# One sink exponential per banded step, a probability copy split between two engines, and final scales at other places of the queue

## The reference, cut to what matters

```python
def swa_core(q, k, v, mask, sink):
    s = jnp.einsum('bnqkgd,bnskd->bnkgqs', q, k).astype(jnp.float32) * (HEAD_DIM ** -0.5)
    s = jnp.where(mask[None, :, None, None], s, -jnp.inf)
    sk = sink.astype(jnp.float32)[None, None, :, :, None, None]
    m = jnp.maximum(jnp.max(s, axis=-1, keepdims=True), sk)
    p = jnp.exp(s - m)
    denom = jnp.sum(p, axis=-1, keepdims=True) + jnp.exp(sk - m)
    w = (p / denom).astype(v.dtype)
    return jnp.einsum('bnkgqs,bnskd->bnqkgd', w, v)

y_prompt = rmsnorm(hp, g_final)
y_sample = rmsnorm(hs, g_final)
```

## Time and profile before

| | us |
|---|---|
| median of 3 runs | 1824.55 (1822.61 to 1825.99) |
| the profiled execution's own time | 1830.64 |
| its span, first to last instruction | 1828.8 |
| PE busy in the span | 1745.8 (95%) |
| DVE, ACT, POOL busy | 879.7, 547.3, 179.6 |
| mean granted TensorE clock | 0.990 |

### The profile page before, as it was taken

How to read it: one execution, slowest core, us unless ns; L and a number is a source line. 1 busy time by engine, 2 the same in 40 slices (tenths; PEclk the granted TensorE clock), 3 DMA queues, 4 the chain that set the end, 5 groups by cost and what they waited for, 6 DMA issues and landing times.

```text
span 1828.8 us, 29483 instructions
## 1 busy us (share of the span) xinstructions
PE 1745.8 (95%) x11905; PEld 1612.9 (88%) x11905; DVE 879.7 (48%) x1707; ACT 547.3 (30%) x1216; POOL 179.6 (10%) x355
## 2 busy tenths in 40 slices
PE   6998989997898999989999999999999999999997
PEld 6997989886787999988799999999999999999996
DVE  5556656665466345124323644444444444444445
ACT  5123344576555123025402422111111222112212
POOL 2113322112122001100000000000000000000002
PEclk9999999999999999999999999999999999999999
DMA  6322322254575406256151101111011111110102
GB/s 214 108 67 60 87 85 87 76 164 163 178 235 205 138 24 247 94 187 226 53 197 47 47 27 43 46 46 46 24 45 46 46 46 46 46 46 25 56 1 104
DMA packets 107533, 170.40 MB, mean 93 GB/s; under 512 B 7545, under 2 KB 75769, under 8 KB 107417
## 3 DMA queue, kind: packets, MB, share of 16 engines
q1 hardware_dynamic: 79512, 126.78, 20.4%
q0 software_dynamic: 8160, 22.29, 3.6%
q10 hardware_dynamic: 19760, 19.92, 3.4%
HBM read 138.17 MB, written 31.72 MB: 93 GB/s over the span
## 4 chain that ended last, share of the span: by engine, by line
PE 87%; DVE 4%; ACT 3%; issue 2%; DMA 2%; POOL 1%; SPq 0%; ACTq 0%; DVEq 0%; POOLq 0%
PE banks L2023 27%; PE banks L1977 24%; PE banks L2412 21%; PE banks L2178 2%; PE banks L2121 2%; PE banks L2300 2%; PE banks L2248 1%; PE banks L1965 1%; PE banks L2208 1%; PE banks L2280 1%; PE banks L2269 1%; ACT probs L1285 1%; DMA w_raw<-in_cache_mem_k 1%; PE banks L2158 1%; DVE xt_lo L1478 1%
## 5 line engine op out<-in xcount | busy, mean ns | idle before, releaser
L1977 PE MATMUL banks<-w_hi,xt_hi 128*128 128x256 f32 x1224 | 354.7, 290 | 17.2 <-DVE xt_lo L1478 4.8
L1977 PE MATMUL banks<-w_lo,xt_hi 128*128 128x256 f32 x1224 | 344.7, 282 | 0.0
L1977 PE MATMUL banks<-w_hi,xt_lo 128*128 128x256 f32 x1224 | 344.5, 281 | 0.0
L2023 PE MATMUL banks<-xt_hi,w_hi 128*128 128x384 f32 x960 | 323.0, 336 | 0.0
L2023 PE MATMUL banks<-xt_hi,w_lo 128*128 128x384 f32 x960 | 322.7, 336 | 0.0
L2023 PE MATMUL banks<-xt_lo,w_hi 128*128 128x384 f32 x960 | 322.6, 336 | 0.0
L1977 PEld LDWEIGHTS banks<-w_hi,xt_hi 128*128 128x128 f32 x1224 | 232.6, 190 | 26.2 <-issue 8.9
L1090 ACT ACTIVATE w_hi<-w_raw 128x2048 fp32r<-128x2048 f32 (+1 forms) x85 | 120.2, 1430 | 418.8 <-PE banks L2412 225.8
L1901 DVE TENSOR_TENSOR h<-h,banks 128x512 f32<-128x512 f32 x288 | 191.9, 683 | 98.9 <-PE banks L2412 96.8
L1977 PEld LDWEIGHTS banks<-w_lo,xt_hi 128*128 128x128 f32 x1224 | 232.9, 190 | 0.0
L1977 PEld LDWEIGHTS banks<-w_hi,xt_lo 128*128 128x128 f32 x1224 | 232.7, 190 | 0.0
(11 more groups left out here) (220 smaller groups left out, 2215.4 us busy)
## 6 DMA issues: line engine op xcount, KB each, us to landing
w_raw<-in_w_up SPq DMA_DIRECT2D x16, 1024.0 KB, 5.4
w_raw<-in_w_down SPq DMA_DIRECT2D x16, 1024.0 KB, 4.9
w_raw<-in_w_xkv ACTq DMA_DIRECT2D x8, 1024.0 KB, 6.1
kc_diff<-in_cache_diff_k SPq DMA_DIRECT2D x16, 512.0 KB, 5.6
vc_diff<-in_cache_diff_v SPq DMA_DIRECT2D x8, 1024.0 KB, 5.4
w_raw<-in_cache_mem_k SPq DMA_DIRECT2D x16, 512.0 KB, 7.6
w_raw<-in_w_in ACTq DMA_DIRECT2D x7, 1024.0 KB, 5.3
scaled<-mix_d SPq DMA_DIRECT2D x9, 512.0 KB, 5.2
```

Of the source, the lines that this page charges most:

```text
L1977: last = mm(out, xt[:, k, tok:tok + P], w[:, k, :], start=(k == 0 and n == 0), stop=(k == KD - 1 and n == 2))
L2023: last = mm(out, w[:, k, :], xt[:, k, tok:tok + CH], start=(k == 0 and n == 0), stop=(k == KD - 1 and n == 2))
```

## The change

It has four edits.

1. A banded step's four sink exponentials become one, behind the second half's exponentials. For it DVE adds the sink to the four negated maxima (`sunk`, four columns) right behind the second half's minimum, and ACT waits for that (`s_sunk`). The streams' banded steps keep theirs.
2. Of a banded step with two groups of turned probabilities (the 14 steps of tiles 1 to 7) ACT copies the first group and DVE the second, in a new function `turned_low_half(i - 2)` between `out_dve(i - 3)` and `combine(i - 1)`. PE then waits for each group at the engine that copies it (`turned_before`).
3. `PREP[39][1]`, group 11 of head 2, goes through bank 1 in place of bank 7, with the waits that this needs.
4. In the last MLP group the final scales of tiles 3 to 7 stand at other places in DVE's queue.

```diff
+GROUPS = [s[0] == "swa" and g == 1 for s in STEPS for g in range(turn_groups(s))]
+V_AT = running(GROUPS)
...
+PREP[I_D2 - 1][1] = (PREP[I_D2 - 1][1][0], 1)
...
                     n = G_AT[i] + g
+                    if GROUPS[n]:
+                        continue
                     src = ps[4 + n % 2]
...
-                        if kind in ("swa", "swas"):
-                            at = 4 * j + 2 * y + g
-                            sk = sink[:, at:at + 1] if kind == "swa" else sink_row[:, :]
-                            last = nc.scalar.activation(esink[:, i % 4, c:c + 1], sk, ACT.Exp, bias=bias)
+                        if kind == "swas":
+                            last = nc.scalar.activation(esink[:, i % 4, c:c + 1], sink_row[:, :], ACT.Exp, bias=bias)
+                    if kind == "swa" and j == 1:
+                        act.wait_ge(s_sunk, SWA_NO[i] + 1)
+                        last = nc.scalar.activation(esink[:, i % 4, 0:4], sunk[:, i % 4, 0:4], ACT.Exp)
...
+                        if kind == "swa" and j == 1:
+
+                            dve.wait_ge(s_negmax, H_AT[i] + 2)
+                            V.tensor_tensor(sunk[:, i % 4, 0:4].rearrange("p (j g) -> p j g", j=2),
+                                            negmax[:, i % 4, 0:4].rearrange("p (j g) -> p j g", j=2),
+                                            sink[:, :].rearrange("p (j n) -> p j n", j=2)[:, :, 2 * y:2 * y + 2],
+                                            ALU.add).then_inc(s_sunk, 1)
...
+            def turned_low_half(i):
+
+                for n in range(G_AT[i], G_AT[i + 1]):
+                    if GROUPS[n]:
+                        dve.wait_ge(s_av, i - 1)
+                        dve.wait_ge(s_pt, n + 1)
+                        V.tensor_copy(turned[:, i % 2, 512:1024], ps[4 + n % 2]).then_inc(s_at_dve, 1)
...
                     if first <= i - 3 < end:
                         out_dve(i - 3)
+                    if first <= i - 2 < end:
+                        turned_low_half(i - 2)
...
-                add_down(g * 3 + 1, odd, 1)
-                add_down(g * 3 + 2, odd, 2, {d: (lambda d=d: final_scale(3 + d // 2)) for d in (1, 3, 5)} if last else None)
+                finals = [{4: lambda: final_scale(3)},
+                          {d: (lambda t=t: final_scale(t)) for d, t in ((0, 4), (2, 5), (4, 6), (5, 7))}]
+                add_down(g * 3 + 1, odd, 1, finals[0] if last else None)
+                add_down(g * 3 + 2, odd, 2, finals[1] if last else None)
...
-            for t in range(6, TT):
-                final_scale(t)
+            final_scale(TT - 1)
...
-                if b < 4 and PREP_LIST[n][0] in range(I_D2, I_X):
+                if b < 4 and PREP_LIST[n][0] in range(I_D2 - 1, I_X):
                     pe.wait_ge(s_exp, halves_on(b, PREP_LIST[n][0]))
```

More of the change, by code:

```diff
@@ L63 @@
 DIFF_NO = {STEP_NO[s]: n for n, s in enumerate(DIFF)}
+SWA_NO = {STEP_NO[s]: n for n, s in enumerate(SWA)}
 I_LAST = STEP_NO[DIFFS[-1]]
@@ L252, in build @@
         esink = sb("esink", [P, 4, 4])
+        sunk = sb("sunk", [P, 4, 4])
         rden = sb("rden", [P, 4, 4])
@@ L418, in build @@
         s_negmax = sem("s_negmax")
+        s_sunk = sem("s_sunk")
         s_exp = sem("s_exp")
@@ L423, in build @@
         s_at = sem("s_at")
+        s_at_dve = sem("s_at_dve")
         s_av = sem("s_av")
@@ L639, in prepared_on @@
         def prepared_on(i, j):
-            on = [n for n, (m, _, b) in enumerate(PREP_LIST) if I_D2 <= m < i < I_X and b in score_banks(i, j)]
-            last = [[n for n in on if (PREP_LIST[n][1][0] == "mem") == low][-1:] for low in (False, True)]
+            on = [n for n, (m, _, b) in enumerate(PREP_LIST) if I_D2 - 1 <= m < i < I_X and b in score_banks(i, j)]
+            last = [[n for n in on if (PREP_LIST[n][1][0] in ("mem", "head")) == low][-1:] for low in (False, True)]
             return [prepared(n) for ns in last for n in ns]
@@ L2218, in scores, with turned_before @@
                     last.then_inc(s_sc, 1)
+            def turned_before(n):
+                if GROUPS[n]:
+                    pe.wait_ge(s_at_dve, V_AT[n + 1])
+                else:
+                    pe.wait_ge(s_at, n + 1 - V_AT[n + 1])
             def turn_probs(i):
@@ L2234, in turn_probs @@
                     if n >= 2:
-                        pe.wait_ge(s_at, n - 1)
+                        turned_before(n - 2)
                     if kind == "swas":
@@ L2252, in values @@
                 kind, x, y = STEPS[i]
-                pe.wait_ge(s_at, G_AT[i + 1])
+                for n in range(G_AT[i], G_AT[i + 1]):
+                    turned_before(n)
                 if i < I_X:
@@ L2361, in _ @@
             attention(*PHASES[0])
-            pe.wait_ge(s_at, G_AT[I_X])
+            turned_before(G_AT[I_X] - 1)
             project_all(Q_OUT, U_OUT, 4, F_MIX, F_N2)
```

## The result

The changed kernel took **1834.55 us** (median of 5 runs, 1833.76 to 1840.36), the kernel before in the same comparison 1825.99 (5 runs, 1822.61 to 1827.82). The ratio is 1.0057, 95% interval 1.0042 to 1.0073: slower, by 7.7 to 13.3 us, where 4.4 us less was forecast, and outside the range.

The account below looks back on a forecast made before the run. TensorE was taken as busy nearly throughout, so ACT or DVE work counts only where PE stands still. The terms -0.8 - 1.7 - 0.5 - 1.4 = -4.4 us took the median from 1824.55 to 1820.1 us, range 1817.0 to 1823.6.

Parts of the forecast that it names:

- the sum: Whole kernel: -0.8 - 1.7 - 0.5 - 1.4 = -4.4 us, giving a median of 1820.1 us.
- all behind it is chained ... and PE goes on: After the banded steps: a shift at 425 us should reach the end, since loads are issued when buffers come free.
- the 0.06 for slower: Rival, chance 0.06: DVE becomes the pace in every banded step, 14 x 0.8 = 11.2 us added, 1831.4 us.
- The sink exponential: Banded steps: PE's waits before steps 17 and 19 shrink by 0.54 and 0.23 us, together -0.8; steps 28 and 29 0.
- Rounds 35 to 40: Up to step 40: DVE's half of the copies and bank 1 for group 11, together -1.7 us, between 0 and -2.4.
- the 1.8 forecast there: `row_max(37)`: 1.8 us sooner, between 0.7 and 1.9, with `values(34)` starting sooner and transposes at full clock.
- the +0.6: Rounds 38 and 39: DVE becomes the pace and each round is 0.3 us longer.
- Round 41: `values(39)` waits 1.77 us for ACT's two copies; one copy less is -0.5 us, bound 0.
- the first 3.0 of the 4.4: Terms ahead of the last scales: sink exponential -0.8, up to step 40 -1.7, round 41 -0.5 us.
- The last scales: End of the program: last scale starts when the last root is ready, near 1818.9, not 1820.27: -1.4 us, -0.5 to -1.6.
- The rival built on it: Rival, chance 0.10: scales of tiles 5 and 6 hold up POOL, the last scale starts where it did: 1821.5 us.
- The gain is lost behind: Rival, chance 0.26: a later wait takes up the banded steps' gain, only the end's 1.4 us is left: 1823.1 us.

Follow-up runs that it names:

- b_pad64: Kernel before plus one unused tensor of 64 bytes per partition behind `esink`, no instruction changed: 1839.83 us, ratio 1.0076.
- a_noshift: The whole change with `sunk` in an unused part of a filler tensor, so every other tensor lies where it lay before: 1828.87 us, ratio 1.0016.
- b_pad32: Kernel before plus one unused tensor of 32 bytes per partition behind `esink`: 1834.7 us, ratio 1.0040.
- b_pad96: Kernel before plus one unused tensor of 96 bytes per partition behind `esink`: 1819.88 us, ratio 0.9956.
- b_xt64: Kernel before with 64 unused bytes ahead of xt and 64 more behind it (xt 64 further, all that follows 128): 1833.26 us, ratio 1.0039.
- b_behind64: Kernel before with 64 unused bytes behind xt only (xt stays, what follows moves 64): 1825.77 us, ratio 0.9998.
- b_hid128: Kernel before with xt, the attention's tensors and third weights 64 bytes further, `sq`, `hid` and `h` 128: 1839.95 us, timed once.
- b_h128: Kernel before with xt and what follows, `sq` and `hid` included, 64 bytes further and only `h` 128: 1837.21 us, timed once.
- a_pad96_hv_act: As a_pad96_hv, but ACT makes both copies of a banded step's turned probabilities again: 1820.55 us, ratio 0.9966 against the kernel before.
- a_pad96: The whole change plus 32 unused bytes behind `sunk`, so all that follows stands 96 bytes further than before: 1824.11 us, ratio 0.9990.
- a_pad96_hv: As a_pad96, with values of heads 8 to 11 counted on separate semaphores, so query and key transposes don't wait for them: 1820.67 us, ratio 0.9972.

## Why the prediction was wrong, point by point

- **The step that failed** is in the sum: that only the rows the edits name change, and "all behind it is chained ... and PE goes on" at its old pace. The sum had no term for the new tensor. `sunk` was costed as one DVE add of 0.2 us; its 64 bytes cost 13.8 us (b_pad64: ratio 1.0076, 1.0059 to 1.0093), three times all the gains forecast. Without the shift (a_noshift) 2.9 of the 8.6 us lost are left. No rival had it either, so the 0.06 for slower went to a mechanism that was not at work: in steps 30 to 34 nothing was lost to DVE (`scores(30)` to `scores(35)` take 35.38 us in a_noshift, 35.37 before).
- **The sink exponential**: -0.8 forecast, between 0 and -1.0. From `scores(16)` to `scores(19)` 18.46 us in a_noshift against 19.55, so -1.1. From `scores(28)` to `scores(30)` nothing was forecast, and 0.1 came (13.33 against 13.40).
- **Rounds 35 to 40**: -1.7 forecast; from `scores(35)` to `scores(40)` the change needs 25.89 us against 27.33, so -1.4, but made up otherwise. `row_max(37)` starts at 391.06 (before 393.33), as said. But 1.1 of the 1.8 forecast there stood for a half-clock stretch, and that belonged to the one execution that was read: that one needs 6.23 us from `scores(36)` to `scores(37)`, while b_pad32, b_pad64, b_pad96, b_xt64, b_behind64, b_hid128 and b_h128, none of which has an edit of the change, need 5.36 or 5.37 (the change 4.61). From `scores(35)` to `scores(40)` these need 26.1 to 27.9, so -1.4 is no firm figure. What was not seen is the load that is late next. And DVE as the pace costs more than the +0.6: PE waits 2.19 ahead of `scores(40)`, and without DVE's copy `scores(40)` follows `scores(39)` 1.1 us sooner (a_pad96_hv_act). What the other bank for group 11 gives by itself, no run shows.
- **Round 41**: the wait fell from 1.77 to 0.48, but `values(39)` starts at 418.90 where it was 418.88, because PE ran at half clock from about 408 to 416 us: its transposes of that time take 1.97 and 1.83 for eight. At the streams' next scores (422.19, before 423.10) -0.9 is left of the first 3.0 of the 4.4, or -1.5 counted from `scores(16)`, which start 0.6 later in the change.
- **The last scales**: -1.4 forecast. From the start of the last group of `features` to the end of the span it is 36.90 us in the change and 38.31 in b_pad64, at the same address: -1.4. The rule of the Trainium skill weighed there ("SBUF — State Buffer", "Who interferes with whom") fits: POOL's last pair, with no scale beside it, takes 0.19 and 0.55. The rival built on it did not come about; a root of 1.42 stood at 1811.50, and the last scale was no later for it.
- **The gain is lost behind** was the rival that described the edits best: without the shift the ratio is 1.0016 (1.0001 to 1.0031), and with the head's load out of the way the medians can't tell them. At the place of the change they may be worth more: it took 1834.55 us against b_pad64's 1839.83, with ratios (1.0057 and 1.0076) whose intervals overlap. The rival's mechanism was half right: new half-clock stretches, but behind a DMA wait, and then loads in the cross-attention.

What stays open: why the place of xt, and of xt against `sq` and `hid`, changes a matmul's pace (shown is only that it does), why the pace behind the cross-attention differs between a_pad96 and a_pad96_hv at one place, and why the same wait is followed by half clock in a_noshift and a_pad96 and not in the change.

## What to carry to other kernels

A change that adds a tensor moves all that is allocated behind it, so list what moves before adding up anything else, and put new scratch into unused room (a_noshift has the pace of before). Compare an edit only with a kernel in which the large matmul operands stand at the same address, and look at the start-to-start time of untouched matmuls first: that tells a change of pace from a wait in one row. Where a chain is shortened, look for the load with the next landing time, and for semaphores that wait for more than the reader reads.

## What the runs showed of the hardware

The pace of a gapless run of matmuls at full clock depends on where its operands begin in SBUF. With xt 0, 32, 64 and 96 bytes further (before, b_pad32, b_pad64, b_pad96: 96, 0, 32 and 64 past a multiple of 128), 256-column matmuls start 117.7, 120.0, 118.3 and 114.0 ns apart in the stretch from 895 to 1020 us, and the 384-column matmuls of the cross queries, whose weights don't move, 173.3, 173.3, 176.7 and 173.3. The place alone does not fix the pace. It can differ by stage: with 96 bytes the same projection line runs at 117.8 ns from 600 to 700 us. It can differ in one stage between two kernels with the same addresses: 117.7 ns in a_pad96 and 114.0 in a_pad96_hv, from 895 to 1020 us. And a product's pace can change when a tensor moves that it does not read (`sq` and `hid`, in b_hid128 and b_xt64: 16.64 and not 16.96 us for 96 matmuls; the tensors behind xt, in b_behind64: 116.7 and not 117.7 ns from 895 to 1020 us). An unused tensor of 96 bytes per partition was worth 0.9956 (0.9939 to 0.9972), more than the runs show for any edit of the change.
